# SwiGLU first projection: gate and up products issued in turns into two PSUM banks

## The reference, cut to what matters

```python
D_MODEL, SEQ, D_FF = 1024, 512, 2816

def _swiglu(x, w1, w2):                      # w1: (1024, 2 * 2816), w2: (2816, 1024)
    gate, up = jnp.split(x @ w1, 2, axis=-1)
    return (jax.nn.silu(gate) * up) @ w2

for l in range(DEPTH):                       # DEPTH = 2
    h = mixer(x)
    x = _layer_norm(ALPHA * x + h, ln1_g[l], ln1_b[l])
    x = _layer_norm(ALPHA * x + _swiglu(x, ffn_w1[l], ffn_w2[l]), ln2_g[l], ln2_b[l])
```

## Time and profile before

| What | us |
|---|---|
| median of three runs | 1502.66 |
| profiled execution: its span, the only time of its own that is shown | 1503.4 |
| TensorE matmuls busy | 1413.9 (94%) |
| GpSimd busy | 528.4 (35%) |
| ScalarE busy | 499.9 (33%) |
| VectorE busy | 480.4 (32%) |

### The profile page before, as it was taken

One profiled execution on the slowest core, in us unless ns is written; L12 is line 12 of the kernel. 1 busy time (PEld: TensorE's weight loads), 2 busy tenths in 40 slices (PEclk: granted clock), 3 DMA queues, 4 the chain that ended last, 5 costly groups with the idle time before them and its releaser, 6 DMA issues.

```text
span 1503.4 us, 19247 instructions
## 1 busy us (share of the span) xinstructions
PE 1413.9 (94%) x7260; PEld 1184.6 (79%) x7260; DVE 480.4 (32%) x1120; ACT 499.9 (33%) x824; POOL 528.4 (35%) x421
## 2 busy tenths in 40 slices
PE   7999996799999999999899998889899999999997
PEld 6888874588888888877878887867779888888776
DVE  3356526553111111014537261633361111110105
ACT  4313236423223232112435554544323323232110
POOL 5421412034444445341342322202234444445350
PEclk9999998899999999999999999979799999999998
DMA  6311121022333333221232121021023333233211
GB/s 217 112 38 48 57 85 56 1 84 61 108 101 96 92 91 112 98 85 29 85 113 57 57 57 57 1 84 56 29 70 91 92 95 102 87 96 113 97 56 56
DMA packets 136323, 117.45 MB, mean 78 GB/s; under 512 B 5412, under 2 KB 112036, under 8 KB 136232
## 3 DMA queue, kind: packets, MB, share of 16 engines
q1 hardware_dynamic: 136232, 116.23, 24.7%
HBM read 114.12 MB, written 2.10 MB: 77 GB/s over the span
## 4 chain that ended last, share of the span: by engine, by line
PE 82%; DVE 8%; ACT 6%; issue 3%; POOL 1%; DMA 0%; ACTq 0%; DVEq 0%; POOLq 0%; SPq 0%
PE banks L448 24%; PE banks L450 24%; PE banks L449 24%; PE banks L870 2%; PE banks L888 2%; PE banks L734 1%; ACT w_hi L985 1%; PE banks L879 1%; POOL w_lo L945 1%; ACT p_fox L1207 1%; PE banks L519 1%; DVE xT_lo L1259 1%; PE banks L834 1%; DVE small L1554 1%; PE banks L801 1%
## 5 line engine op out<-in xcount | busy, mean ns | idle before, releaser
L945 POOL TENSOR_TENSOR w_lo<-w_raw,w_hi 128x512 fp32r<-128x512 f32 x417 | 528.2, 1299 | 936.6 <-ACT w_hi L985 936.6
L448 PE MATMUL banks<-xT_lo,w_hi 128*128 128x512 f32 (+2 forms) x928 | 347.0, 374 | 2.5 <-DVEq L1261 2.4
L449 PE MATMUL banks<-xT_hi,w_lo 128*128 128x512 f32 (+2 forms) x928 | 344.7, 371 | 0.0
L450 PE MATMUL banks<-xT_hi,w_hi 128*128 128x512 f32 (+2 forms) x928 | 344.6, 371 | 0.0
L985 ACT ACTIVATE w_hi<-w_raw 128x2048 fp32r<-128x2048 f32 (+1 forms) x107 | 200.0, 1869 | 213.1 <-PE banks L450 177.7
L448 PE MATMUL banks<-w_lo,xT_hi 128*128 128x512 f32 (+1 forms) x608 | 222.6, 366 | 10.6 <-ACT o_fox L1007 3.9
L450 PE MATMUL banks<-w_hi,xT_hi 128*128 128x512 f32 (+1 forms) x608 | 215.0, 354 | 0.0
L449 PE MATMUL banks<-w_hi,xT_lo 128*128 128x512 f32 (+1 forms) x608 | 215.0, 354 | 0.0
L448 PEld LDWEIGHTS banks<-xT_lo,w_hi 128*128 128x128 f32 (+1 forms) x928 | 175.6, 189 | 32.5 <-issue 3.3
L450 PEld LDWEIGHTS banks<-xT_hi,w_hi 128*128 128x128 f32 (+1 forms) x928 | 175.4, 189 | 30.1
L449 PEld LDWEIGHTS banks<-xT_hi,w_lo 128*128 128x128 f32 (+1 forms) x928 | 175.6, 189 | 29.2
(11 more groups left out here) (167 smaller groups left out, 1285.5 us busy)
## 6 DMA issues: line engine op xcount, KB each, us to landing
w_raw<-in_ffn_w_dram SPq DMA_DIRECT2D x92, 512.0 KB, 4.0
w_raw<-in_ffn_w_dram SPq DMA_DIRECT2D x20, 1024.0 KB, 4.9
w_raw<-in_fox_w_in_dram SPq DMA_DIRECT2D x16, 1024.0 KB, 5.8
w_raw<-in_even_w_in_dram SPq DMA_DIRECT2D x14, 1024.0 KB, 5.0
w_raw<-in_even_w_out_dram SPq DMA_DIRECT2D x4, 1024.0 KB, 5.1
w_raw<-in_fox_w_out_dram SPq DMA_DIRECT2D x4, 1024.0 KB, 6.4
x_res<-in_x_dram SPq DMA_DIRECT2D x4, 512.0 KB, 8.1
out_dram<-x_res SPq DMA_DIRECT2D x4, 512.0 KB, 2.6
```

The lines of the kernel that those rows point to most:

```text
L448: mm(acc, l_hi, r_lo, start=first, stop=False)
L449: mm(acc, l_lo, r_hi, start=False, stop=False)
L450: return mm(acc, l_hi, r_hi, start=False, stop=final)
L945: ins = nc.gpsimd.tensor_tensor(w_lo[c % RING][:, a:a + n], w_raw[c % RAW][:, a:a + n], w_hi[c % RING][:, a:a + n].bitcast(F32), ALU.subtract)
```

## The change

In chunks 2 to 21 of both layers the two banks are opened together, and for each of the 8 feature blocks the six matmuls are issued as gate, up, gate, up, gate, up: high by low into both banks, low by high into both, high by high into both. Each bank receives the same 24 matmuls in the same order as before. The gate bank is closed by the last matmul but one of the chunk, the up bank by the last. The semaphores, the bank order and the work of the other engines are as they were. Chunks 0 and 1 (`up_product`) are not touched.

```diff
                     weights_in(c)
-                    for part in range(2):
-                        key = (f"up{l}", j, part)
-                        acc = open_bank(key, next_gemm_bank(), "act" if part == 0 else "dve")
-                        for k in range(KD):
-                            a = part * KD * P + k * P
-                            ins = products(acc[:, :], hi(c, a, P), lo(c, a, P), xT_hi[:, k, :],
-                                           xT_lo[:, k, :], k == 0, k == KD - 1)
-                        close_bank(key, ins)
+                    pair = [open_bank((f"up{l}", j, part), next_gemm_bank(), "act" if part == 0 else "dve")
+                            for part in range(2)]
+                    for k in range(KD):
+                        first, final = k == 0, k == KD - 1
+                        at_w = [part * KD * P + k * P for part in range(2)]
+                        for acc, a in zip(pair, at_w):
+                            mm(acc[:, :], hi(c, a, P), xT_lo[:, k, :], start=first, stop=False)
+                        for acc, a in zip(pair, at_w):
+                            mm(acc[:, :], lo(c, a, P), xT_hi[:, k, :], start=False, stop=False)
+                        for part, (acc, a) in enumerate(zip(pair, at_w)):
+                            key = (f"up{l}", j, part)
+                            ins = mm(acc[:, :], hi(c, a, P), xT_hi[:, k, :], start=False, stop=final)
+                            if final:
+                                close_bank(key, ins)
                     used_with_bank(c, key)
```

## The result

| | kernel before | kernel after |
|---|---|---|
| median, us (five runs each) | 1502.66 (1501.79 to 1504.18) | 1508.67 (1506.58 to 1512.94) |
| ratio to before, 95% interval | | 1.0040 (1.0026 to 1.0054) |
| span of the profiled execution, us | 1503.4 | 1504.8 |

The change makes the kernel slower by 6.0 us (3.9 to 8.1). The two profiled executions differ by only 1.4 us. The one after is the fastest of its five, 2.1 us under its median. Its span of 1504.8 us belongs to a run of 1506.58 us, so 1.8 us lie outside a span. With the same 1.8 us the profiled execution of before took about 1505.2 us (an estimate), 2.5 us over its median. A comparison by stage is needed.

What follows compares the result with a forecast made beforehand. The prediction took TensorE's queue as the bound (82% of the chain of waits). Two stalls of 2.64 and 2.63 us plus 1.6 us of clock made 6.9 us, so 1509.5 us against the median, range 1504 to 1513.

Steps and rivals of the forecast that it cites:

- Part 1, the turns cost and give nothing: Up stages of both layers, 1920 products alternating between two banks: spacing stays 0.2267 us, effect zero; bounds -25.7 and +154 us.
- two thirds of the turns' gain: Rival's partial size: alternating banks shortens up-stage products, giving two thirds of at most 25.7 us, 1485 to 1490; chance 0.08.
- Inside the stage PE doesn't notice: Up stage: silu and weight rounding move 5.21 us later, but 8.25 us spare leaves 3.04, so no wait on PE.
- At the stage's end it does: Second down chunk, behind a half chunk: late w_lo stalls PE, costing 2.64 us in layer 0 and 2.63 in layer 1.
- silu about 0.3 us behind the chunk's end: Sign in the up stage's profile: ACT's silu starts there instead of at the chunk's middle.
- The clock: Behind each new second-down-chunk stall, TensorE may fall to 1.2 GHz for 3.4 us, costing 0 or 1.6 us; chance 0.54 each.
- one drop: Likeliest count of clock falls behind the two new stalls, 1.6 us in all; chance 0.42 with the stalls.
- the term of 1.6 us: Cost of one half-clock stretch behind a new down-stage stall: 8 products, each 0.20 us longer.
- The sum: Whole kernel: 2.64 + 2.63 + 1.6 = 6.9 us slower, 1510.3 us on the profiled execution, 1509.5 against the median.
- the case without a drop: Rival: same two stalls at the second down chunks, clock stays up, 5.3 us slower, 1508.0; chance 0.18.

## Why the prediction was right

- *Part 1, the turns cost and give nothing.* Right to the last digit: 0.2267 us in 2 x 960 spacings. The rows at single changes of bank in the trace of before did carry over to steady alternation. Two slips did no harm. The working says that two of each three neighbours already share their moving operand; it is one pair in three before (`xT_lo`, `xT_hi`, `xT_hi`) and two in three after, and the spacing didn't change with it. And two thirds of the turns' gain would have given 1502.66 - 17.1 + 5.3 = 1491, not 1485 to 1490.
- *Inside the stage PE doesn't notice.* Right: no wait in either up stage, and 38 turned chunks cost nothing.
- *At the stage's end it does.* Right in place, releaser and size: 2.64 us predicted, 2.57 in the profile. The stall was there in all three kernels in which the rounding waits for a late gate and a half chunk follows, and in none of the others. The sign "silu about 0.3 us behind the chunk's end" was off: its own figures give 581.20 + 5.21 - 586.38 = 0.03, which is what was measured; 0.3 was the delay of VectorE.
- *The clock.* The new stalls behaved as the count had it, and the sum of the clock's losses did not. In each of the three profiles with new stalls (the changed kernel, only the last chunk turned, gate second) the one in layer 1 was followed by a stretch at 1.2 GHz and the one in layer 0 was not, so "one drop" fits. But each of the three also lost one: behind the old late stall of layer 1 the clock was 0.50 in the earlier trace rows, and here it stays at its upper level. PE's rows of the changed kernel:

```profile
1468.45 0.47 PE L448 MATMUL banks<-w_lo,hT_hi 128*128 128x512 f32 x1 [1.81 <-POOL w_lo L951]
1468.75 0.39 PE L449 MATMUL banks<-w_hi,hT_lo 128*128 128x512 f32 x1
1468.98 0.40 PE L450 MATMUL banks<-w_hi,hT_hi 128*128 128x512 f32 x1
```

  And the stretches behind the same stall with the columns of the earlier trace rows, only the last chunk turned and then gate second:

```profile
1469.90:1473.30 3.40, 3.40 (x15) 2.81 (x16) 0.29 (x1) 0.00 (x0) 0.00 (x0) 1.00 0.00 0
1470.22:1473.62 3.40, 3.40 (x15) 2.81 (x16) 0.28 (x1) 0.00 (x0) 0.00 (x0) 1.00 0.00 0
```

  In the table by stage both lie in the last row, the new drop (+1.5) and the lost one (-1.6), and leave -0.07. So in the profiles the term of 1.6 us came to nothing in this place. A new idle time moves all later ones, and that another drop might go with it I had only in the range, not in the sum. The late drop is not tied to the new stalls alone: the profile with the half chunk moved has none of them and lost it too.
- *The sum.* 1509.5 predicted, 1508.67 measured; 1508.0 was the case without a drop. The two stalls were right, 2 x 2.57 = 5.1 us (5.6 with the gate second). The three kernels with the stalls were 6.0, 5.7 and 5.5 us slower than before in their medians. What is over the stalls, 0.9 us or less, is within the intervals (some 2 us either way), so the medians can't tell a clock term of nothing from one of 1.6 us; that the forecast lies as near as 0.8 us is in part luck. One place where the rest may lie is the mixer of layer 1: it took 433.8 to 433.9 us in the three profiles with new stalls, and 431.5 to 433.0 in the five without them and with the same second half of the down stage (the kernel before, all but the last turned, the two with early rounding, the half chunk moved). With one profile each, it is not shown whether that is a late effect of the stalls or scatter. One step of the working was off without harm: I set the profiled execution of before 0.7 us over the median by its span, but with the 1.8 us outside a span it was some 2.5 us over.

## What to carry to other kernels

Before issuing two accumulations in turns, ask when each closes and who starts work on that event: here nothing on TensorE changed, and the whole cost came from an in-order ScalarE list in which the rounding of weights stood behind the silu of a bank that now closes late. The place to look is where the consumer's step is shortest: the half-size chunk right behind the stage takes 5.44 of the 8.25 us of spare time that a chunk has inside it, and it decides alone. Work that does not depend on the late event goes ahead of the wait for it, and a half-size chunk belongs where its short preparation is of use, not where its short run is a deadline.

## What the runs showed of the hardware

A 128 x 512 product costs 0.2267 us whether it adds into the bank of the product ahead or into another one, at every product, 0.0134 us over half the 0.4267 us of the lower clock. Changing the bank doesn't take that remainder away; what holds it was not tested.

The length of an idle time alone didn't decide whether the clock fell. Stalls of one length (2.34 us, 2.56 with the gate second) were followed by 1.2 GHz in layer 1 and not in layer 0, in three profiles. The old stall of 1.81 us in layer 1 was followed by it in four profiles (the kernel before, all but the last turned, the two with early rounding) and not in four others (the changed kernel, only the last turned, gate second, the half chunk moved).

Executions of one kernel scatter by several us, and mostly with the mean granted clock: of the turned kernel with the early rounding, the four runs at 0.967 took 1501.2 to 1501.9 us, and the three at 0.961 took 1505.7 to 1507.0. The clock is not all of it: two runs of the changed kernel at 0.965 took 1506.6 and 1511.0. Part of what a profile of one execution seems to gain or lose is this, so the stages need to be lined up before a difference of 1 to 5 us is given to an edit.
